# Two of four output-gate projection tiles moved from the matrix-LSTM stage into the attention stage of a hybrid decoder layer

## The chip, the core and the metric

The kernel runs on one core of one Trainium2 chip. The metric is the device time of one execution in microseconds; lower is better. The engines are TensorE (PE, its weight loads shown apart as PEld), VectorE (DVE), ScalarE (ACT), GpSimd (POOL) and SyncE (SP, which here only issues DMAs).

## The reference

One decoder layer over 1,024 positions of width 1,024, float32, batch 1. The attention has 8 heads of 64 (compressed, selected and window keys), the matrix-LSTM 4 heads of 128. The input is normalised and projected by one matrix of 3,360 columns; two groups of heads use parts of the result, are joined and projected back, and a memory attention and a gated MLP follow.

```python
h = rmsnorm(x, g_mix[l])
(nq, nkc, nvc, nks, nvs, nkw, nvw, ngt, mq, mk, mv, mo, mi, mf) = split_cols(h @ w_in[l], IN_SIZES)
o_nsa = nsa_batched(nq, ...)
qk = jax.nn.silu(causal_dwconv(jnp.concatenate([mq, mk], axis=-1), mlstm_conv_w[l]))
mq, mk = jnp.split(qk, 2, axis=-1)
h_m = mlstm_chunkwise(hd4(mq), hd4(mk), hd4(mv), mi + mlstm_b_i[l], mf + mlstm_b_f[l])
mixed = jnp.concatenate([head_rmsnorm(o_nsa, g_head_nsa[l]),
                         jax.nn.sigmoid(mo) * head_rmsnorm(h_m, g_head_mlstm[l])], axis=-1)
x = x + mixed @ w_out[l]
```

The part that matters here is `mo`: 512 columns, 128 for each of the four matrix-LSTM heads, whose sigmoid gates the normalised head. It depends on `h` alone, so it may be computed at any time after `h`.

## The kernel before

**Tiles.** Every projection is cut into tiles of 128 output columns. A tile of weights is loaded by SP (`load`, one of two slots in turn), split by POOL into a high and a low part (`split_tile`, L848 and L851) and multiplied on PE by the high and low parts of `h`, which stay in SBUF. One k-step of one half (512 positions) is three matmuls in `product` (L994, L997, L998); a tile is 2 halves x 8 k x 3 matmuls (`gemm_tile`). The order of the tiles is written by hand in `weight_tiles`, and all engines count along the same order with semaphores. POOL may overwrite a slot's split weights when PE has begun the tile after (`tile_started`); SP may load into a raw slot when its former tile is split.

**PSUM.** There are 8 banks of 512 columns. A ring hands them out: PE waits for `chunk_freed` before it opens a bank that is used again, DVE raises it when it has copied a bank out. During the attention the ring rests: scores use banks 0 to 3, transposes 4 and 5, sums 6 and 7.

**Attention (149 to 450 us of the span).** 128 head scores (4 heads x 2 branches x 16 blocks) and 164 steps (transposes of probabilities with the sums by values, and 16 turns of outputs) are interleaved in `NSA_ORDER`, an order made at build time from buffer space and a lag in columns; all engines walk it. For a score: PE `score_head` (L1144 to L1153) -> DVE maximum `shift_head` (L2196) -> ACT exponential `exp_head` (L1602) -> DVE reciprocal (L2208) -> POOL scaling (L876). PE may score head j when head j-2 has been exponentiated. For a step: PE four transposes `turn_block` (L1173, outputs L1164) -> ACT high part (L1622) -> DVE low part (L2004) -> PE two sums `sum_block` (L1192, L1193). The order begins with scores 0 to 9, one turn, score 10, two turns, scores 11 and 12. The last score (127) is followed by eleven steps, 153 to 163, of which 162 and 163 turn outputs and wait for a copy by ACT.

**Matrix-LSTM heads (450 to 700 us).** For each head PE runs the tiles of q, k, v and output gate in this order, then transposes `mv_feat` (L1035) as soon as DVE has copied the v tile, then the products of q and k in 12 pieces (L994 to L998 again, on `mq` and `mk`), then 72 matmuls of 129 columns with `tri` (L1250). DVE runs for q and for k: copy out (L2282), convolution over four taps (L2285, L2287), and after ACT's silu the low part (`mq_lo`, `mk_lo`, L2005); then `mv_feat` (L2301), the mask of the diagonal blocks (L2308), the copy of the output-gate tile into `o_gate` (L2311), the copy of the transposed v (L2314), and the pieces of `tri` (L2326, L2331) with decays that ACT makes (L1666, L1673). Then the head is normalised. ACT takes the sigmoid of `o_gate` behind the decays (L1676). `o_gate` lies over the keys of the attention, so nothing can be written there before the attention ends. Head 3 has 32 more transposes, of the attention's output, before its `tri` matmuls. The first 11 weight tiles are loaded before the attention begins; at its start the tile for head 0's q is split already, the one for k is loaded.

## Time and profile before

| | us |
|---|---|
| median of 3 runs | 1812.86 |
| lowest and highest run | 1810.57, 1812.99 |
| the profiled execution, its time | 1812.26 |
| its span (first to last instruction) | 1810.4 |

| engine | busy us | share of the span |
|---|---|---|
| PE | 1715.0 | 95% |
| PEld | 1417.8 | 78% |
| DVE | 1229.9 | 68% |
| ACT | 708.3 | 39% |
| POOL | 860.0 | 48% |

The profile is of one execution. Its page gives totals, the span in 40 slices and the costliest groups; the timeline gives each instruction with its start, its duration and, in brackets, how long its engine was idle before it and what released it. Starts are from the span's begin. Matmuls overlap: the duration of one is longer than the distance to the next, so distances between starts are used for sums. PEclk is the granted clock of PE as a share of 2.4 GHz.

### The profile page before, as it was taken

The page shows a single profiled execution, that of the slowest core. Times are in us where ns is not written, and L with a number is a line of the kernel's source. Part 1 is how long each engine was busy: PE and PEld are TensorE (multiplying, and loading weights), DVE is VectorE, ACT ScalarE, POOL GpSimd, SP SyncE. Part 2 cuts the span into 40 slices and gives each one's busy share as a digit, 9 for nine tenths or more (in the row PEclk, how much of TensorE's full clock was granted, in tenths as well). Part 3 has the DMA queues.
Part 4 walks back from the last instruction along what each step waited for, and adds up shares of the span by engine and source line. Part 5 has one row for each costly group of instructions (what it writes and reads, how often), then busy time and mean ns, then how long its engine had stood idle before and what let it go on. Part 6 is the DMA issues. An engine that isn't in the chain of part 4 may idle for free.

```text
span 1810.4 us, 23333 instructions
## 1 busy us (share of the span) xinstructions
PE 1715.0 (95%) x8416; PEld 1417.8 (78%) x8416; DVE 1229.9 (68%) x1641; ACT 708.3 (39%) x1326; POOL 860.0 (48%) x659
## 2 busy tenths in 40 slices
PE   7998899999999999989999898999999999999997
PEld 6886788877888887778777687777888888877886
DVE  6754677775887776446443532877888788789965
ACT  5114677776223324134111202433444443543444
POOL 3333344443433231410222243458988888679851
PEclk9998999998999999989999899999999999999999
DMA  5230011010111113114101022125533544695342
GB/s 189 82 117 13 24 36 36 28 44 1 58 47 36 36 59 128 47 38 151 57 23 35 24 82 93 35 82 199 191 125 120 175 144 144 207 330 181 118 133 93
DMA packets 78595, 170.07 MB, mean 94 GB/s; under 512 B 7644, under 2 KB 24220, under 8 KB 78368
## 3 DMA queue, kind: packets, MB, share of 16 engines
q1 hardware_dynamic: 67944, 135.71, 23.1%
q10 hardware_dynamic: 10552, 33.05, 4.8%
q8 instruction: 60, 0.98, 0.2%
q14 instruction: 39, 0.32, 0.1%
HBM read 133.06 MB, written 35.67 MB: 93 GB/s over the span
## 4 chain that ended last, share of the span: by engine, by line
PE 56%; DVE 17%; POOL 10%; ACT 7%; issue 7%; DMA 1%; ACTq 0%; SPq 0%; DVEq 0%; POOLq 0%
PE ps L994 13%; PE ps L998 13%; PE ps L997 13%; DVE x_t L2529 4%; PE ps L1173 3%; ACT x_t L1831 2%; POOL sum_s L905 2%; PE ps L1250 2%; POOL w_lo L899 2%; PE ps L1144 2%; PE ps L1334 2%; POOL w_lo L955 2%; DVE x_t L2558 2%; PE ps L1192 2%; DVE h_lo L2005 2%
## 5 line engine op out<-in xcount | busy, mean ns | idle before, releaser
L994 PE MATMUL ps<-h_hi,w_hi 128*128 128x512 f32 x1108 | 442.3, 399 | 17.2 <-DVE h_lo L2004 5.9
L997 PE MATMUL ps<-h_lo,w_hi 128*128 128x512 f32 x1108 | 436.8, 394 | 0.0
L998 PE MATMUL ps<-h_hi,w_lo 128*128 128x512 f32 x1108 | 436.8, 394 | 0.0
L848 POOL TENSOR_TENSOR w_hi<-w_raw,ones 128x1024 fp32r<-128x1024 f32 x55 | 113.9, 2070 | 619.2 <-PE ps L994 516.8
L994 PEld LDWEIGHTS ps<-h_hi,w_hi 128*128 128x128 f32 x1108 | 211.2, 191 | 71.1 <-ACT p_sum L1800 7.1
L998 PEld LDWEIGHTS ps<-h_hi,w_lo 128*128 128x128 f32 x1108 | 211.2, 191 | 44.8
L997 PEld LDWEIGHTS ps<-h_lo,w_hi 128*128 128x128 f32 x1108 | 211.7, 191 | 43.0 <-issue 0.7
L876 POOL TENSOR_SCALAR probs<-probs,nsa_inv,gate_sig 128x640 f32<-128x640 f32 (+7 forms) x128 | 100.2, 783 | 172.3 <-DVE nsa_inv L2208 172.3
L2529 DVE SCALAR_TENSOR_TENSOR x_t<-ps,par,x_t 128x1023 f32<-128x1023 f32 x84 | 107.7, 1282 | 80.2 <-ACT x_t L1831 78.7
L851 POOL TENSOR_TENSOR w_lo<-w_raw,w_hi 128x1024 fp32r<-128x1024 f32 x55 | 147.3, 2679 | 4.3
L2004 DVE TENSOR_TENSOR pt_lo<-ps,pt_hi 128x512 fp32r<-128x512 f32 (+1 forms) x148 | 101.8, 688 | 57.9 <-ACT pt_hi L1622 55.9
L1173 PE MATMUL ps<-ident,probs 128*128 128x128 f32 (+1 forms) x592 | 96.3, 288 | 12.1 <-POOL probs L876 6.6
L1622 ACT ACTIVATE pt_hi<-ps 128x512 fp32r<-128x512 f32 (+1 forms) x148 | 87.7, 596 | 45.8 <-PE ps L1173 45.1
L1602 ACT ACTIVATE probs<-ps,nsa_shift 128x640 f32<-128x640 f32 (+7 forms) x128 | 89.8, 702 | 38.6 <-DVE nsa_shift L2196 21.5
L2196 DVE TENSOR_REDUCE nsa_shift<-ps 128x1 f32<-128x640 f32 (+7 forms) x128 | 88.9, 698 | 16.2 <-PE ps L1153 11.2
L1173 PEld LDWEIGHTS ps<-ident,probs 128*128 128x128 f32 (+1 forms) x592 | 65.4, 141 | 25.2 <-DVE pt_lo L2004 11.1
L1144 PE MATMUL ps<-k_a,q_st 128*128 128x512 f32 (+3 forms) x192 | 71.2, 371 | 12.0 <-ACT probs L1602 7.5
L1710 ACT ACTIVATE sq<-x_t 128x1024 f32<-128x1024 f32 x16 | 17.0, 1061 | 147.0 <-DVE x_t L2373 80.5
L1760 ACT ACTIVATE xp<-ps,shift 128x256 f32<-128x256 f32 x32 | 15.0, 471 | 136.8 <-DVE shift L2473 136.8
L2004 DVE TENSOR_TENSOR z_lo<-h_part,z_hi 128x512 fp32r<-128x512 f32 x40 | 59.1, 1493 | 12.1 <-ACT z_hi L1878 12.1
L1145 PE MATMUL ps<-k_a,q_st 128*128 128x512 f32 (+3 forms) x192 | 65.7, 348 | 0.0
L899 POOL TENSOR_TENSOR w_lo<-w_raw,w_hi 128x512 fp32r<-128x512 f32 x38 | 51.4, 1352 | 29.3 <-ACT w_hi L1818 29.3
(360 smaller groups left out, 4079.2 us busy)
## 6 DMA issues: line engine op xcount, KB each, us to landing
w_raw<-in_w_tiles SPq DMA_DIRECT2D x109, 512.0 KB, 3.6
w_raw<-in_w_tiles SPq DMA_DIRECT2D x55, 256.0 KB, 3.0
s_new<-in_w_tiles SPq DMA_DIRECT2D x44, 256.0 KB, 4.0
z_dram<-x_t ACTq DMA_DIRECT2D x21, 512.0 KB, 2.9
b<-z_dram SPq DMA_DIRECT2D x33, 256.0 KB, 4.1
q_st<-q_dram SPq DMA_DIRECT2D x64, 128.0 KB, 2.9
t_dram<-t_new ACTq DMA_DIRECT2D x22, 256.0 KB, 5.2
s_dram<-s_new SPq DMA_DIRECT2D x22, 256.0 KB, 2.8
```

The costliest lines, as they stand in the source:

```text
L848: pool.tensor_tensor(w_hi[s][:, :], w_raw[s][:, :], ones[:, :].to_broadcast([P, KT * P]), ALU.mult).then_inc(w_hi_made.sem, w_hi_made.up())
L851: pool.tensor_tensor(w_lo[s][:, :], w_raw[s][:, :], w_hi[s][:, :].bitcast(FP32), ALU.subtract).then_inc(weights_split.sem, weights_split.up())
L876: ins = pool.tensor_scalar(row, row, nsa_inv[:, j % 8, br:br + 1], gate_sig[:, i, 3 * h + 1 + br:3 * h + 2 + br], ALU.mult, ALU.mult)
L994: ins = mm(out_ap, whi, x_hi, start=first, stop=False)
L997: mm(out_ap, whi, x_lo, start=False, stop=False)
L998: return mm(out_ap, wlo, x_hi, start=False, stop=last)
L1144: mm(o, qa, k_a[br][:, g, at_key:at_key + m], start=True, stop=False)
L1173: last = transpose(ps[0:width, 4 + k % 2, hd * P:hd * P + P], probs[:, at_p:at_p + width], ident[:, :])
L1602: ins = f(probs[:, P_AT[j]:P_AT[j] + n], flat[:, 0:n], ACT.Exp, bias=nsa_shift[:, j % 8, br:br + 1], accum_out=nsa_sums[:, j % 8, br:br + 1])
L2004: return tt(out_lo, src, hi.bitcast(FP32), ALU.subtract)
L2196: ins = dve.tensor_reduce(nsa_shift[:, j % 8, br:br + 1], flat[:, 0:n], AX.X, ALU.max, negate=True)
L2529: ins = stt(fc[p][i][:, k:SEQ], ps_flat[:, b:b + SEQ - k], conv_f[:, FTAPS - 1 - k, n:n + 1], fc[p][i][:, k:SEQ], ALU.mult, ALU.add)
```

## The change

The weight order becomes: output gates of heads 3 and 2 first, directly ahead of head 0's q; heads 0 and 1 keep four tiles, heads 2 and 3 have three.

The tile of head 3 is computed in eight portions (two k each, `fill_first`) in PSUM bank 7, behind scores 1, 2, 3, 4 (first half) and 6, 7, 8, 9 (second half). DVE copies each half, scaled, into `first_o`, behind its reductions of scores 6 and 11; PE starts the second half only after the first copy. `first_o` lies over a part of `o_nsa`, so ACT sends it by DMA to DRAM behind score 14, and from there into `o_gate` behind the attention.

The tile of head 2 is split by POOL in the middle of the attention (high part behind scaling 40, low part behind scaling 60), computed in eight portions (`fill_second`) in banks 0 and 1 behind steps 154 to 161, and copied by DVE into `o_gate` at the start of the matrix-LSTM stage.

```diff
+LAST_SCORE = max(n for n, (what, _) in enumerate(NSA_ORDER) if what == "s")
+FILL_AT = {1: (0, 0), 2: (0, 2), 3: (0, 4), 4: (0, 6), 6: (1, 0), 7: (1, 2), 8: (1, 4), 9: (1, 6)}
...
+    for h in (3, 2):
+        columns(win, C_MO + h * P)
     for h in range(MH):
-        for c in (C_MQ, C_MK, C_MV, C_MO):
+        for c in (C_MQ, C_MK, C_MV) + ((C_MO,) if h < 2 else ()):
...
+        first_o = at("first_o", FREE + 62 * KB, [P, SEQ])
+        o_dram = nc.dram_tensor("o_dram", (P, SEQ), FP32)
...
+                if j == 40:
+                    high_tile(0)
+                if j == 60:
+                    low_tile(0)
+
-            split_tile(0)
             split_pairs((FIRST_KV - 11) // 2)
...
+            def fill_second(c, k0, k1, slot):
+
+                for k in range(k0, k1):
+                    w = (w_hi[slot][:, k * P:k * P + P], w_lo[slot][:, k * P:k * P + P])
+                    ins = product(ps[:, c, :], w, h_hi[:, k, c * HALF:c * HALF + HALF], h_lo[:, k, c * HALF:c * HALF + HALF],
+                                  k == 0, k == KT - 1, tag=(c == 0 and k == 0))
+                if k1 == KT:
+                    ins.then_inc(chunk_done.sem, chunk_done.up())
+
+            fill_done = t("fill_done")
+            fill_slot = next_weights()
+
+            def fill_first(c, k0, k1):
+
+                if c and not k0:
+                    pe.wait_ge(t("fill_copied").sem, c)
...
+                    ins = product(ps[:, 7, :], w, h_hi[:, k, c * HALF:c * HALF + HALF], h_lo[:, k, c * HALF:c * HALF + HALF],
+                                  k == 0, k == KT - 1, tag=(c == 0 and k == 0))
...
+                if br == 0 and a == 0 and job == 1:
+                    pe.wait_ge(t("fill_copied").sem, 2)
...
                     score_head(z)
+                    if z in FILL_AT:
+                        c, k = FILL_AT[z]
+                        fill_first(c, k, k + 2)
...
+                    if at_order == LAST_SCORE + 2:
+                        fill_slot = next_weights()
+                        ring.resize(8)
+                        pe.wait_ge(head_exped.sem, HEADS)
+                    if LAST_SCORE + 2 <= at_order < LAST_SCORE + 10:
+                        n = at_order - LAST_SCORE - 2
+                        fill_second(n // 4, n % 4 * 2, n % 4 * 2 + 2, fill_slot)
...
-                gemm_tile(h_hi, h_lo)
-
-                pe.wait_ge(chunk_freed.sem, chunk_done.value(4))
+                if h < 2:
+                    gemm_tile(h_hi, h_lo)
+
+                pe.wait_ge(chunk_freed.sem, chunk_done.value(4 if h < 2 else 2))
...
+                    if z == 14:
+                        act.wait_ge(t("fill_copied").sem, 2)
+                        act.dma_start(o_dram[:, :], first_o[:, :]).then_inc(t("fill_moved", 16).sem, 16)
...
             act.wait_ge(ssq_ready.sem, ssq_ready.next())
+            act.wait_ge(t("fill_moved", 16).sem, 16)
+            act.dma_start(o_gate[:, 3, :], o_dram[:, :]).then_inc(t("fill_moved", 16).sem, 16)
...
+                if h == 3:
+                    act.wait_ge(t("fill_moved", 16).sem, 32)
...
+                    if g == 0 and i in (3, 4):
+                        dve.wait_ge(t("fill_moved", 16).sem, 16)
...
+            def copy_first(c):
+                dve.wait_ge(t("fill_done").sem, c + 1)
+                cs = slice(c * HALF, c * HALF + HALF)
+                tt(first_o[:, cs], ps[:, 7, :], r_in[:, cs], ALU.mult).then_inc(
+                    t("fill_copied").sem, t("fill_copied").up())
...
                     shift_head(n)
+                    if n in (6, 11):
+                        copy_first(n // 11)
...
+            b = chunk(2)
+            tt(o_gate[:, 2, :], both(b), r_in[:, :], ALU.mult).then_inc(chunk_freed.sem, chunk_freed.up(2))
             for h in range(MH):
...
-                b = chunk(2)
-                tt(o_gate[:, h, :], both(b), r_in[:, :], ALU.mult).then_inc(chunk_freed.sem, chunk_freed.up(2))
+                if h < 2:
+                    b = chunk(2)
+                    tt(o_gate[:, h, :], both(b), r_in[:, :], ALU.mult).then_inc(chunk_freed.sem, chunk_freed.up(2))
```

The eight semaphores `x_loaded0` to `x_loaded7` are given up, to make room for new ones; the loads of x use `block_loaded0` to `block_loaded7` instead, whose later values count one more.

## Rows read from the trace of the kernel before

**Rows 1.** The page, busy time of each engine and its share of the span
```profile
PE 1715.0 (95%) x8416; PEld 1417.8 (78%) x8416; DVE 1229.9 (68%) x1641; ACT 708.3 (39%) x1326; POOL 860.0 (48%) x659
```

**Rows 2.** Windows: length, busy PE, PEld, DVE, ACT, POOL, then PEclk, DMA share, GB/s
```profile
170.00:200.00 30.00, 22.79 (x138) 19.68 (x137) 17.34 (x44) 16.46 (x48) 10.53 (x16) 0.89 0.07 18
...
500.00:560.00 60.00, 60.00 (x318) 51.58 (x317) 45.84 (x70) 17.35 (x23) 19.09 (x8) 1.00 0.14 45
```

**Rows 3.** Timeline of PE, first scores: scores 2 and 10, and turn of step 3
```profile
153.87 0.33 PE L1144 MATMUL ps<-k_a,q_st 128*128 128x128 f32 x1 [2.68 <-ACT probs L1602]
...
165.85 0.50 PE L1144 MATMUL ps<-k_a,q_st 128*128 128x512 f32 x1 [0.54 <-ACT probs L1602]
...
174.87 1.09 PE L1173 MATMUL ps<-ident,probs 128*128 128x128 f32 x4 [3.77 <-POOL probs L876]
```

**Rows 4.** Windows; the last two of PE alone: length, busy PE, PEclk, DMA share, GB/s
```profile
154.00:158.00 4.00, 3.77 (x18) 3.58 (x18) 1.22 (x8) 1.63 (x9) 1.76 (x4) 0.51 0.01 2
...
444.00:448.00 4.00, 2.44 (x12) 0.95 0.00 0
...
450.00:454.00 4.00, 4.00 (x10) 0.50 0.00 0
```

**Rows 5.** Timeline of DVE, the reduction of a 128-column score
```profile
158.28 0.29 DVE L2196 TENSOR_REDUCE nsa_shift<-ps 128x1 f32<-128x128 f32 x1 [0.79 <-PE ps L1153]
```

**Rows 6.** Timeline of PE: step 154, step 162, head 0's first tile
```profile
435.81 0.60 PE L1173 MATMUL ps<-ident,probs 128*128 128x128 f32 x4
436.16 0.48 PE L1192 MATMUL ps<-pt_hi,v_hl 128*128 128x512 f32 x1
436.48 0.40 PE L1193 MATMUL ps<-pt_lo,v_hl 128*128 128x512 f32 x1
...
445.26 0.63 PE L1164 MATMUL ps<-ident,o_turn 128*128 128x128 f32 x4 [0.78 <-ACT o_turn L1630]
...
449.82 0.79 PE L994 MATMUL ps<-h_hi,w_hi 128*128 128x512 f32 x1 [0.93 <-DVE o_nsa L2218]
...
456.19 0.39 PE L994 MATMUL ps<-h_hi,w_hi 128*128 128x512 f32 x1
...
477.27 0.39 PE L994 MATMUL ps<-h_hi,w_hi 128*128 128x512 f32 x1
```

**Rows 7.** Timeline of DVE in head 1
```profile
534.08 1.23 DVE L2005 SCALAR_TENSOR_TENSOR mq_lo<-u_conv,mq_hi 128x1024 fp32r<-128x1024 f32 x1 [2.22 <-ACT mq_hi L1663]
...
546.26 1.95 DVE L2005 SCALAR_TENSOR_TENSOR mk_lo<-u_conv,mk_hi 128x1024 fp32r<-128x1024 f32 x1 [2.22 <-ACT mk_hi L1663]
548.14 1.21 DVE L2301 TENSOR_TENSOR mv_feat<-ps,r_in 128x1024 f32<-128x1024 f32 x1
549.28 3.19 DVE L2308 SCALAR_TENSOR_TENSOR u_conv<-m_bc,log_in,mmask 128x128 f32<-128x128 f32 x8
555.92 1.23 DVE L2311 TENSOR_TENSOR o_gate<-ps,r_in 128x1024 f32<-128x1024 f32 x1 [3.46 <-PE ps L998]
```

**Rows 8.** Timeline of PE in head 1: first product of q and k, then `tri`
```profile
556.45 0.47 PE L994 MATMUL ps<-mq_hi,mk_hi 128*128 128x512 f32 x1
...
563.10 8.26 PE L1250 MATMUL ps<-mv_tok,tri 128*128 128x129 f32 x72
```

**Rows 9.** Timeline of ACT and its DMA queue in heads 1 and 2
```profile
552.50 1.06 ACT L1666 ACTIVATE u_conv<-u_conv 128x1024 f32<-128x1024 f32 x1 [4.97 <-DVE u_conv L2308]
553.46 1.22 ACT L1673 ACTIVATE decay<-m_bc,log_in 128x384 f32<-128x384 f32 x2
...
579.75 0.33 ACTq L1657 DMA_DIRECT2D m_bc<-m_dram  x1
```

**Rows 10.** Timeline of POOL: scalings 41 and 61, first half of a split
```profile
247.43 0.98 POOL L876 TENSOR_SCALAR probs<-probs,nsa_inv,gate_sig 128x768 f32<-128x768 f32 x1 [1.41 <-DVE nsa_inv L2208]
...
291.44 0.88 POOL L876 TENSOR_SCALAR probs<-probs,nsa_inv,gate_sig 128x640 f32<-128x640 f32 x1 [2.24 <-DVE nsa_inv L2208]
...
545.24 1.89 POOL L848 TENSOR_TENSOR w_hi<-w_raw,ones 128x1024 fp32r<-128x1024 f32 x1 [5.72 <-PE ps L994]
```

More of the change, by code:

```diff
@@ L525, in build @@
             names[f"down_loaded{i}"] = ctx.enter_context(nc.semaphore(f"down_loaded{i}"))
-        for i in range(TT):
-            names[f"x_loaded{i}"] = ctx.enter_context(nc.semaphore(f"x_loaded{i}"))
         class View:
@@ L841, in _, with high_tile @@
             hi_made = w_hi_made
-            def split_tile(s):
+            def high_tile(s):
                 pool.wait_ge(loaded[s].sem, loaded[s].next())
@@ L849, in split_tile, with low_tile @@
                     w_hi_made.sem, w_hi_made.up())
+            def low_tile(s):
                 pool.wait_ge(w_hi_made.sem, w_hi_made.value())
@@ L853, in split_tile @@
                 tile_started.add(1)
+            def split_tile(s):
+                high_tile(s)
+                low_tile(s)
             def split_pairs(turns):
@@ L1115, in _ @@
             assert ring.bank() == FIRST_BANK
+            def fill_second(c, k0, k1, slot):
[10 more added lines that the diff above has]
+                    pe.wait_ge(t("fill_copied").sem, c)
+                for k in range(k0, k1):
+                    w = (w_hi[fill_slot][:, k * P:k * P + P], w_lo[fill_slot][:, k * P:k * P + P])
+                    ins = product(ps[:, 7, :], w, h_hi[:, k, c * HALF:c * HALF + HALF], h_lo[:, k, c * HALF:c * HALF + HALF],
+                                  k == 0, k == KT - 1, tag=(c == 0 and k == 0))
+                if k1 == KT:
+                    ins.then_inc(fill_done.sem, fill_done.up())
             def score_head(j):
@@ L1196, in _ @@
             summed = 0
-            for what, z in NSA_ORDER:
+            for at_order, (what, z) in enumerate(NSA_ORDER):
                 if what == "s":
                     score_head(z)
+                    if z in FILL_AT:
+                        c, k = FILL_AT[z]
+                        fill_first(c, k, k + 2)
                 else:
@@ L1511, in x_high @@
             def x_high(k):
-                act.wait_ge(t(f"x_loaded{k}", 16).sem, t(f"x_loaded{k}", 16).next())
+                act.wait_ge(t(f"block_loaded{k}", 16).sem, t(f"block_loaded{k}", 16).next())
                 f(h_hi[:, k, :], x_f[:, k, :], ACT.Copy, scale=gains[:, G_MIX, k:k + 1]).then_inc(
@@ L1655, in _ @@
             ring.resize(8)
+            chunk_done.add(2)
             for h in range(MH):
@@ L1663, in _ @@
                     f(hi[:, :], u_conv[:, :], ACT.Copy, scale=scale).then_inc(hi_ready.sem, hi_ready.up())
-                chunk_done.add(8 + 2 + 2 + (2 if h else 0))
+                chunk_done.add((8 if h < 2 else 6) + 2 + 2 + (2 if h else 0))
                 act.wait_ge(diag_ready.sem, diag_ready.next())
@@ L1868, in down_highs @@
                     block_loaded = t(f"block_loaded{k}", 16)
-                    block_loaded.n = {0: 1, 1: 2, 3: 3, 5: 5, 6: 4}[n]
+                    block_loaded.n = {0: 1, 1: 2, 3: 3, 5: 5, 6: 4}[n] + (k < KT)
                     act.wait_ge(block_loaded.sem, block_loaded.value())
@@ L2602, in z_sum @@
                 block_loaded = t(f"block_loaded{k}", 16)
-                block_loaded.n = 3 if n == 2 else 4
+                block_loaded.n = (3 if n == 2 else 4) + (k < KT)
                 dve.wait_ge(block_loaded.sem, block_loaded.value())
```

5 lines of the change are left out of this document (2 added, 3 removed).

## The prediction

> **What bounds the kernel now.** I read the page's totals first: TensorE (PE) is busy 95% of the span, VectorE (DVE) 68% [rows 1]. A change that moves PE work pays only if it moves it from where PE is the limit to where PE waits. So next comes the table by stretches [rows 2]: at the start of the attention PE is busy 22.8 of 30 us; in the matrix-LSTM heads 60.0 of 60, and DVE 45.8.
>
> The change takes one of the four projection tiles out of heads 2 and 3, where PE never rests, and lays both tiles into the attention. Two questions decide: how much of each tile falls into gaps there, and whether a head without it is shorter by the whole tile or meets another wait first. They need PE's timeline at both places of the attention [rows 3, 6] and DVE's, PE's and ACT's in a head [rows 7 to 9].
>
> **Price of a tile.** 93 matmuls of 512 columns, 31 groups of three, start between 456.19 and 477.27 [rows 6]: 0.227 us each. A tile is 2 halves x 8 x 3 = 48 of them, 10.9 us; a portion of two k is 6, 1.36 us, and twice that where the granted clock is 0.5.
>
> **First tile, eight portions behind scores 1 to 4 and 6 to 9.** Score 2 starts at 153.87 after 2.68 us of waiting for ACT [rows 3]; the portion behind score 1 fits into that wait and is free. From 154 to 158 PE is busy 3.77 us of 4, at a granted clock of 0.51, that is 1.2 GHz [rows 4]: hardly a gap is left, only slow matmuls. Score 10 starts at 165.85, 12.0 us behind score 2; less 0.54 of waiting [rows 3], 0.5 for the turn before it and some 0.3 of smaller gaps that is 10.7 of slow scores, 5.3 at full clock.
> The new length: scores 5.3, seven portions 9.5, the turn 0.5. PE is idle most of the time until 153.87 still, so I let the clock fall at 154 and come back after one dense portion: 1.6. The portion behind score 6 needs the bank that DVE empties only after it has reduced score 6: 0.29 and a little more for the reduction [rows 5], 0.6 to 0.7 for a 128x512 copy (half of the 1.21 of a 128x1024 one, [rows 7]), with the hand-overs 1.4 in which PE waits; score 7 and all behind it stand in its queue. Sum 18.3 against 12.0: +6.3. The second copy stands on DVE between the reductions of scores 11 and 12, ahead of the reciprocal that POOL, and then the turn at 174.87 with its idle time of 3.77, wait for [rows 3]: +0.5. For a further short fall of the clock in the copy wait, +0.7. First tile **+7.5**. Ends: +3.3 (no fall of the clock, copy wait hidden) and +10.9 (nothing hidden). I see nothing later that absorbs it: in the attention PE, ACT, DVE and POOL wait for one another, and so shift together.
>
> **Second tile, eight portions behind the last turns.** A turn is four transposes (0.35), then two sums (0.32, and some 0.24) [rows 6]: 0.91. From 435.81 to 445.26, less the 0.78 of waiting before it, there are eight steps, 1.08 each, so only 0.17 a step and those 0.78 are open. From 436.9 there remain 7 x 0.91 = 6.4 plus 10.9: the turn of 445.26 moves to 454.2, **+8.9**. The tail, 445.26 to 449.82 [rows 6], stays. In it PE was busy 2.44 of 4 us, and from 450 to 454 head 0's first tile ran at a granted clock of 0.50 [rows 4], a loss of 2. Behind denser work it may fall later: I take off 0.9. Second tile **+8.0**; ends +6.7 and +10.9. It also puts one DVE copy of 1.2 ahead of head 0, where its banks are emptied. That costs nothing, since DVE waits 3.46 us for the output-gate tile in head 0 as in head 1 [rows 7]; without that cover it would cost 1.2.
>
> **POOL and DMAs.** The second tile's split goes behind POOL's scalings 40 and 60. POOL idles 1.41 us ahead of scaling 41 and 2.24 ahead of 61; the first half of a split takes 1.89 (545.24), the second I bound by twice that [rows 10]. So a scaling starts up to 1.5 us late and the next, with idle times of their own, are on time: 0, at most 2. The split for head 0's first tile may start once the second tile has started, 17 us ahead of need. The two DMA issues on ACT cost about 0.33 of its queue each (a like issue, [rows 9]), the second ahead of the root that DVE waits for, but under the cover of head 0. The data are back long before head 3. Together **+0.3**. SP loads one tile per split as before, in another order of columns.
>
> **Heads 2 and 3 without their tile.** In head 1 DVE reads the fourth tile at 555.92 [rows 7], so the third ends at about 545.0. DVE ends mv_feat, which frees the third tile's bank for PE's transposes, at 549.35, works to 552.5 on the mask, idles 3.46 for the fourth tile, copies it (1.15) and goes on [rows 7]. Without the tile PE waits for mv_feat. POOL's split from 545.24 [rows 10], beside which mk_lo takes 1.95 where mq_lo takes 1.23 [rows 7], moves up to the third tile's start: 0.7 gained. DVE gains 3.46 + 1.15 + 0.7 = 5.3, less 0.45, as ACT's first decay is ready only 1.6 us behind the mask (552.50 to some 554.1, [rows 9]): the products that fill tri start 4.85 earlier. PE's 72 small matmuls behind them [rows 8], held by DVE first and dense after, end some 5.1 earlier, not 10.9. In head 3 the part before them hangs on DVE wholly: 4.8. Together **-9.9**; ends -7 and -21.8. Half of each removed tile turns into PE waiting for DVE.
>
> **Sum.** 7.5 + 8.0 + 0.3 - 9.9 = +5.9. The profiled execution took 1812.26 us, 1.9 more than its span of 1810.4; the median of three runs is 1812.86, 0.6 above it. 1812.3 + 5.9 = **1818.2**.
>
> **A rule weighed.** The rows say: 2.68 us idle, then a granted clock of 0.51; 2.44 busy of 4 until 448, then 0.50 [rows 3, 4]. The Trainium skill, "TensorE: Matmul & The Clock Gate", Part 1, says that the throttled state is the default and activity releases it. For the first tile this speaks for the change: the portions would hold the clock up, and the sum would be the second rival's. For heads 2 and 3, with a new idle time of about 4 us, it speaks against it: the third rival's.
>
> **Rivals.**
> 1. *Heads bound by PE.* PE shows 60.0 of 60 busy [rows 2]. If DVE's chain closes up once the tiles come sooner, both tiles vanish whole: 7.5 + 8.0 + 0.3 - 21.8 = -6.0, 1806.3. It decides where mv_feat ends less than 1 us behind the third tile; against it, it ends 4.4 behind. Chance 0.13.
> 2. *The clock stays up.* The first portion fills the wait before 153.87, the scores run at 2.4 GHz and the copy wait is half hidden: first tile +4.0, second +6.9, sum +1.3, 1813.6. For it: the half-rate stretch is there to be won. Against: 2.44 busy of 4 did not hold the clock at 448 [rows 4]. Chance 0.24.
> 3. *New falls of the clock.* After the idle time in heads 2 and 3 the products ahead of tri (6.65 us from 556.45 to 563.10, [rows 8]) run at half rate and DVE waits for them; the copy wait lowers the clock in the scores again: savings -7, first tile +10, sum +11.3, 1823.6. For it: shorter waits than those 4 us lowered the clock at 154 and 450 [rows 4]. Against: DVE and ACT take the products at a slower pace than PE makes them, so they have a lead to lose. Chance 0.18.
> 4. The forecast, 0.45.
>
> **How the numbers follow.** About 0.2% (3.6 us) is what a measurement can tell from no change. Rival 1 and a sliver of 2 are faster: 0.15. Most of rival 2 and a sixth of the forecast, whose open terms spread it by some 3 us each way, are within: 0.29. The rest is slower: 0.56. The range goes from the forecast to rival 2's better side and rival 3's centre, leaving out rival 1 and the top of rival 3: 1810 to 1824.5.
>
> **What would show it.** Right: score 10 starts 5 to 8 us later; head 0's first tile starts at about 465; the output-gate copies of heads 0 and 1 stay 60 apart, the heads 2 and 3 take about 55; PE idles 4 us before the transposes of mv_feat there, released by DVE. Wrong: granted clock 1.0 from 154 to 162 (rival 2); a head of about 49 us (rival 1); clock 0.5 under the products of heads 2 and 3 and DVE waiting for PE (rival 3).

## The result and the profile after

The changed kernel took 1822.43 us (median) beside 1812.72 for the kernel before: a ratio of 1.0056, 95% interval 1.0031 to 1.0080. Five of its six executions lie at 1821.91 to 1823.82; the sixth took 2155 us at a mean granted clock of 0.747 and is left out of the ratio. In a later session it was 1821.05 beside 1811.54, ratio 1.0053 (1.0041 to 1.0066). So it is some 10 us slower, where the forecast said +5.9 and 1818.2, with a range to 1824.5. It moved the way that was forecast and ended inside the range. The size was 4 us short, and the runs below show which terms made that up.

The page's busy times, to be laid beside [rows 1]. The work is the same; DVE has one operation more, as the first tile is copied in two halves.

```profile
PE 1715.6 (94%) x8416; PEld 1417.5 (78%) x8416; DVE 1229.8 (68%) x1642; ACT 708.3 (39%) x1326; POOL 859.8 (47%) x659
```

The span is 1820.5 against 1810.4. I followed the offset between the two traces at matching operations, that is, how much later the same operation starts in the changed kernel:

| place (time before) | after less before | step |
|---|---|---|
| score 1 (150.64) | +1.2 | ahead of any portion |
| score 10 (165.85) | +6.1 | first tile, its portions: +4.9 |
| turn of step 3 (174.87) | +6.5 | |
| DVE's low part 24 (224.25) to 437 | +11.4 to +11.8 | what came behind it: +5.2 |
| head 0's first tile (449.82) | +20.8 | second tile: +9.1 |
| o_gate tile of head 1 (555.92) | +23.8 | head 0: +3.0, head 1: 0 |
| end of head 2 | +18.4 | -5.4 |
| end of head 3 | +12.3 | -6.1 |
| end | +10.1 | -2.2 |

Below, an offset "at step 8, 12 or 24" is that of DVE's low part of this number (at 185, 196 and 224 us in before); a "turn" is PE's.

Timeline of PE in the changed kernel, for [rows 3]: score 2, the first matmul of the tile's second half, score 10, the turn of step 3.

```profile
155.12 0.33 PE L1180 MATMUL ps<-k_a,q_st 128*128 128x128 f32 x1 [1.26 <-ACT probs L1650]
...
163.24 0.49 PE L1007 MATMUL ps<-h_hi,w_hi 128*128 128x512 f32 x1 [1.11 <-DVE first_o L2286]
...
172.00 0.48 PE L1180 MATMUL ps<-k_a,q_st 128*128 128x512 f32 x1
...
181.34 1.09 PE L1209 MATMUL ps<-ident,probs 128*128 128x128 f32 x4 [3.87 <-POOL probs L886]
```

The first portion lay in the wait (1.26 left of 2.68), the second half waited 1.11 us for the copy, and PE's wait for POOL before step 3 is as long as ever. Windows of PE alone, for [rows 4] (length, busy PE, granted clock, DMA share, GB/s):

```profile
154.00:158.00 4.00, 2.88 (x16) 1.00 0.01 2
158.00:162.00 4.00, 4.00 (x28) 1.00 0.02 4
182.00:186.00 4.00, 4.00 (x15) 0.50 0.00 0
186.00:190.00 4.00, 4.00 (x18) 0.56 0.00 0
```

The clock stays at 2.4 GHz where it was 0.51 before, but behind the wait for POOL it is at or near 1.2 GHz for some eight us, where the profile of before shows one window of four at 0.57 (below, with experiment 6). At the end of the attention, where [rows 4] have 2.44 busy of 4 us and then 0.50, it does not fall: PE is busy 2.29 of 4 us from 467 to 471, and the clock reads 1.00 there and in the four behind. The end of the attention, for [rows 6]: step 162 and head 0's first tile.

```profile
466.57 0.60 PE L1200 MATMUL ps<-ident,o_turn 128*128 128x128 f32 x4
...
470.64 0.50 PE L1007 MATMUL ps<-h_hi,w_hi 128*128 128x512 f32 x1 [0.93 <-DVE o_nsa L2276]
```

Head 0, on ACT's queue, on DVE and on PE, with a window of PE behind its wait. This is the stretch that the prediction had down as covered.

```profile
479.53 0.33 ACTq L1705 DMA_DIRECT2D o_gate<-o_dram  x1
479.89 1.28 ACT L1706 ACT_TABLE_LOAD   x1 [9.77 <-DVE ssq L2311]
```
```profile
481.48 0.55 DVE L2315 RECIPROCAL rstd<-rstd 128x64 f32<-128x64 f32 x1 [1.98 <-ACT rstd L1706]
482.06 8.81 DVE L2318 TENSOR_TENSOR o_nsa<-o_nsa,rstd 128x512 f32<-128x512 f32 x8
...
516.56 1.22 DVE L2369 TENSOR_TENSOR mv_feat<-ps,r_in 128x1024 f32<-128x1024 f32 x1
...
519.79 1.22 DVE L2380 TENSOR_TENSOR o_gate<-ps,r_in 128x1024 f32<-128x1024 f32 x1
```
```profile
517.84 1.97 PE L1048 MATMUL ps<-ident,mv_feat 128*128 128x128 f32 x8 [3.38 <-DVE mv_feat L2369]
```
```profile
517.00:521.00 4.00, 3.17 (x12) 0.57 0.00 0
```

For head 0 of the kernel before, the line that answers to the o_gate copy:

```profile
495.90 1.22 DVE L2311 TENSOR_TENSOR o_gate<-ps,r_in 128x1024 f32<-128x1024 f32 x1 [3.47 <-PE ps L998]
```

DVE now reaches the o_gate tile with no wait at all, where it waited 3.47 us before, as in head 1 [rows 7]. PE waits 3.38 us for mv_feat in a head that still has all four tiles, and the clock falls to 1.2 GHz behind that wait. The cover, the waiting of DVE in which the prediction hid the copy and the issues, was used up.

Head 2, the DVE operations that answer to [rows 7], and PE's wait:

```profile
630.09 1.23 DVE L2061 SCALAR_TENSOR_TENSOR mk_lo<-u_conv,mk_hi 128x1024 fp32r<-128x1024 f32 x1 [2.21 <-ACT mk_hi L1717]
...
632.37 2.18 DVE L2376 SCALAR_TENSOR_TENSOR u_conv<-m_bc,log_in,mmask 128x128 f32<-128x128 f32 x8
...
636.25 0.29 DVE L2395 TENSOR_TENSOR tri<-ps,u_conv 128x128 f32<-128x128 f32 x1 [0.50 <-ACT decay L1727]
```
```profile
632.51 1.30 PE L1048 MATMUL ps<-ident,mv_feat 128*128 128x128 f32 x8 [3.77 <-DVE mv_feat L2369]
```

Here the forecast's picture stands: mk_lo takes 1.23 where it took 1.95, the wait of 3.46 and the copy are gone, ACT's first decay costs 0.50, and PE idles 3.77 us for DVE. The mask too lost the split on POOL that ran beside it (2.18 for 3.19), which the forecast had left out.

### The profile page after: what moved, and what is told of

The parts are those of the page before. It is cut to its first block, busy times and chain, and to the rows that moved or that the text cites. A ratio compares the mean times of both kernels' runs of the same rounds, so it can differ in the third digit from the quotient of the medians.

```text
span 1820.5 us, 23339 instructions
## 1 busy us (share of the span) xinstructions
PE 1715.6 (94%) x8416; PEld 1417.5 (78%) x8416; DVE 1229.8 (68%) x1642; ACT 708.3 (39%) x1326; POOL 859.8 (47%) x659
## 4 chain that ended last, share of the span: by engine, by line
PE 50%; DVE 21%; POOL 10%; ACT 8%; issue 8%; DMA 1%; ACTq 0%; SPq 0%; DVEq 0%; POOLq 0%
PE ps L1007 11%; PE ps L1010 11%; PE ps L1011 11%; DVE x_t L2598 4%; PE ps L1209 3%; ACT x_t L1887 2%; POOL sum_s L918 2%; DVE u_conv L2355 2%; POOL w_lo L912 2%; PE ps L1382 2%; DVE x_t L2627 2%; DVE h_lo L2061 2%; PE ps L1180 2%; PE ps L1230 2%; POOL w_lo L968 1%
## 5 line engine op out<-in xcount | busy, mean ns | idle before, releaser
L1209 PE MATMUL ps<-ident,probs 128*128 128x128 f32 (+1 forms) x592 | 97.3, 289 | 12.3 <-POOL probs L886 6.9
L1209 PEld LDWEIGHTS ps<-ident,probs 128*128 128x128 f32 (+1 forms) x592 | 66.8, 143 | 24.7 <-issue 11.4
L1180 PE MATMUL ps<-k_a,q_st 128*128 128x512 f32 (+3 forms) x192 | 70.1, 365 | 9.6 <-ACT probs L1650 5.4
L1230 PE MATMUL ps<-pt_hi,v_hl 128*128 128x512 f32 x132 | 65.0, 493 | 0.0
```

The source lines that it names most:

```text
L1180: mm(o, qa, k_a[br][:, g, at_key:at_key + m], start=True, stop=False)
L1209: last = transpose(ps[0:width, 4 + k % 2, hd * P:hd * P + P], probs[:, at_p:at_p + width], ident[:, :])
L1230: mm(o, v, pt_hi[k % 3][0:e, :], start=br == 0 and a == 0, stop=False)
```

## The experiments

Theory at the start: the parts of the table above add up, each with its price. Rivals: that what came behind score 10 is not the tile's but the clock's, drawn anew in each execution; that head 0's loss is the order on ACT's queue. Ratios are against the kernel before on the same chip, with 95% intervals.

**1. The first tile alone** (head 3's tile; head 2 computes its own again; no copy of a gate ahead of head 0, head 0's split back behind the scalings).

```
-    for h in (3, 2):
+    for h in (3,):
...
-                if h < 2:
+                if h not in (3,):
                     gemm_tile(h_hi, h_lo)
```

> The changed kernel with head 3's output-gate tile alone moved (between the first scores, copied to DRAM and back); head 2 computes its own as before, nothing is laid between the last turns, POOL splits head 0's first tile after its last scaling as before. Theory (the parts add up as the trace of after reads): +10.5 in the attention, of which 6 stand at score 10 and the rest comes from longer falls of the clock by step 40, head 3 -6, head 0 at nothing because its wait for the o_gate tile is back: +4.5 against before, between +3 and +6. Rival (the rest beyond score 10 is how the falls of the clock happen to lie in one execution, not the price of the tile): offset at score 10 of 5 to 6 and no more behind, total -1 to +1.

Measured: 1815.98, ratio 1.0030 (1.0017 to 1.0043), +5.4 us or so. Attention +11.1, head 0 to 1 +1.8, head 3 -5.6, all against the first profile of before. The total lies in the theory's range, but head 0 was not at nothing: PE waits there without a second tile in the kernel. The rival is out by its total; by experiment 6 it was right about 4 of the 11.1.

```profile
506.80 1.97 PE L1045 MATMUL ps<-ident,mv_feat 128*128 128x128 f32 x8 [2.54 <-DVE mv_feat L2357]
```

**2. The second tile alone** (the same edits for head 2, without the first tile and its two DMAs).

```
-                    if z in FILL_AT:
-                        c, k = FILL_AT[z]
-                        fill_first(c, k, k + 2)
...
-            act.dma_start(o_gate[:, 3, :], o_dram[:, :]).then_inc(t("fill_moved", 16).sem, 16)
```

> Head 2's output-gate tile alone moved, between the last turns; the first scores are those of before, and no DMA of a gate. Theory: +9.0 in the last turns, head 0 at 0 to +1.3 (the copy of the gate ahead of it, mostly under its 3.46 us of waiting, which the second tile's place leaves there), head 2 -5.4: +4.3, between +3.5 and +5.5; the attention's steps up to 435 us as before within 1. Rival A (the tile's price is the clock: head 0's first tile ran at half rate before and does not now): +7 in the turns, total +2. Rival B (head 0 is the place where it is lost, whatever was moved first): head 0 +3 again, total +7.

Measured: 1818.78, ratio 1.0053 (1.0036 to 1.0069), +9.6 by the ratio, more than any theory said. The profiled execution was the quickest of the six, 1816.06; in it the turns cost +9.6 and head 2 gave 4.3 back. Its surprise is at the start: with nothing of the change in the first scores, it stands -0.4 at score 10, +2.9 at step 8, +4.8 at step 24 and +5.0 by 250 us against the first profile of before. That is the growth of the changed kernel, +5.2 from score 10 to step 24. So it is not the tile's.

**3. The load behind the root.**

```
-            act.wait_ge(t("fill_moved", 16).sem, 16)
-            act.dma_start(o_gate[:, 3, :], o_dram[:, :]).then_inc(t("fill_moved", 16).sem, 16)
             f(rstd[:, :, 0:NH], ssq[:, :, 0:NH], ACT.Sqrt, scale=1.0 / DH, bias=EPS).then_inc(
                 std_ready.sem, std_ready.up())
+            act.wait_ge(t("fill_moved", 16).sem, 16)
+            act.dma_start(o_gate[:, 3, :], o_dram[:, :]).then_inc(t("fill_moved", 16).sem, 16)
```

> The changed kernel with one edit: ACT issues the load of o_gate from DRAM behind the root of the NSA norms, not ahead of it. Theory: the root comes 1.3 to 1.65 us earlier, and as head 0 now has no wait left on DVE, all behind it comes as much earlier; the scaling of o_nsa also no longer lies beside the load: 1.5 to 3 us faster than the changed kernel, so +7 to +8.5 against before. Rival A (the root hides under another wait, POOL's split or PE): no difference to the changed kernel, +9 to +10. Rival B (the slow scaling of o_nsa is POOL's split beside it, so it stays 8.8 us): only the 1.65 are gained.

Measured: 1819.99, ratio 1.0051 (1.0029 to 1.0073): no gain by the median. The profile (an execution of 1812.53) shows what the order does, on ACT and on DVE:

```profile
476.18 0.26 ACT L1704 ACTIVATE rstd<-ssq 128x64 f32<-128x64 f32 x1 [8.10 <-DVE ssq L2311]
476.19 0.33 ACTq L1707 DMA_DIRECT2D o_gate<-o_dram  x1
```
```profile
476.47 0.56 DVE L2315 RECIPROCAL rstd<-rstd 128x64 f32<-128x64 f32 x1 [0.32 <-ACT rstd L1704]
477.06 8.80 DVE L2318 TENSOR_TENSOR o_nsa<-o_nsa,rstd 128x512 f32<-128x512 f32 x8
```

The root's table load is no longer in the chain and the wait is 0.32 as it was before, 1.66 less. The scaling still takes 8.80 (rival B), and it does in experiment 2 too, where no gate is loaded. Its eight operations, read one at a time, show why: six take 0.68 or 0.69 each, and two take this:

```profile
480.69 2.38 DVE L2318 TENSOR_TENSOR o_nsa<-o_nsa,rstd 128x512 f32<-128x512 f32 x1
...
482.99 2.88 DVE L2318 TENSOR_TENSOR o_nsa<-o_nsa,rstd 128x512 f32<-128x512 f32 x1
```

They are the two beside the halves of POOL's split, which lie at 480.39 (2.13 us) and 482.60 (2.72). Every profile with a scaling of 8.80 has exactly one such pair, and it moves with the split. In before (4.91) the split starts at 463.46, when six of the eight are done; the last two take 0.69, and here the split's first half is the long one, 2.79. No PE wait for mv_feat is left in head 0 here.

This profile's span is 10.3 us below the changed kernel's, but that is not all the order's: 3.6 lie in head 0, 2.3 near 435 us, where the clock did not fall in this execution, and 4.2 behind head 3.

**4. Six spare matmuls in the first wait**, into a bank that nobody reads.

```
                     score_head(z)
+                    if z == 1:
+                        pe.wait_ge(weights_split.sem, weights_split.n + 1)
+                        for k in range(2):
+                            w = (w_hi[1][:, k * P:k * P + P], w_lo[1][:, k * P:k * P + P])
+                            product(ps[:, 7, :], w, h_hi[:, k, 0:HALF], h_lo[:, k, 0:HALF], k == 0, k == 1)
```

> The kernel before with six matmuls more behind score 1, into a bank that nobody reads there: they take 1.4 us of a wait of 2.7 us. They move nothing. Theory (the wait lets the clock fall to half, and work in it holds the clock up): granted clock 1.0 from 154 to 162, score 10 some 4 to 5 us earlier; of this 0 to 4 us arrive at the end, as later falls of the clock take some of it back. Rival A (the clock falls for what PE did before 138, not for this wait): no difference. Rival B (the cost of first falls is given back wholly by ACT's and DVE's own pace behind score 10): score 10 earlier, the end the same within 1.

Measured: 1811.74, ratio 1.0010 (0.9998 to 1.0021): nothing. The granted clock read 0.91 from 154 to 158 and 0.50 from 158 to 162: the fall came 3 us later, not never. Score 10 stood 0.9 earlier, and later falls took that back (+2.3 by 250 us). One portion in the wait does not hold the clock; in the changed kernel each following score had its portion, and there it held. A finding by the way: this kernel has nothing of the change in head 0, but its first tile runs there at full clock, and of DVE's wait for the o_gate tile 0.43 is left.

```profile
495.87 1.23 DVE L2316 TENSOR_TENSOR o_gate<-ps,r_in 128x1024 f32<-128x1024 f32 x1 [0.43 <-PE ps L998]
```

**5 and 6. Both kernels a second time, unedited.**

> The changed kernel once more, unedited, on the chip of the runs below, for a second profile of the same program. Theory (when the clock falls is drawn anew in each execution, and the offset of +11.7 in the attention held some of it): against the profile of before the score 10 stands +4 to +6 again, but the steps behind it and the tail differ from the first profile by up to 3 us where a fall lies elsewhere; PE's wait for mv_feat in head 0 is there again. Rival (the falls belong to the program): each offset the same within 0.5.

> The kernel before once more, unedited, for a second profile. Theory: head 1 to the end of head 3 the same within 0.5; between 154 and 240 us the steps later than in the first profile by 2 to 5 us, as they are in the kernels that share this code (the one with the second tile alone, +5.1; the one with six spare matmuls, +2.3), or the first dense head at full clock where the first profile showed it at half. Rival (those offsets came from the edits): each step the same within 0.5.

Measured: the changed kernel 1821.05, the one before 1811.67 (ratio to itself 0.9999, 0.9989 to 1.0009). Windows of PE alone in the second profile of **before**:

```profile
154.00:158.00 4.00, 3.04 (x16) 0.67 0.01 2
178.00:182.00 4.00, 4.00 (x15) 0.50 0.00 0
194.00:198.00 4.00, 3.94 (x17) 0.50 0.02 4
222.00:226.00 4.00, 4.00 (x15) 0.50 0.02 4
```

The same stretches in the first profile of before, the one with the forecast's rows:

```profile
174.00:178.00 4.00, 3.13 (x11) 0.57 0.00 0
190.00:194.00 4.00, 2.00 (x8) 0.70 0.20 59
214.00:218.00 4.00, 1.86 (x7) 0.69 0.00 0
```

One program has a window wholly at 1.2 GHz after each of three waits in one execution, and a shorter fall each time in the other. It stands +4.2 by step 24 and keeps that to the end of the heads, though its total is 0.8 less than the first's (it lost less elsewhere). The second profile of the changed kernel stands +11.0, so the second pair differs by 6.8 where the first pair differs by 11.7. What follows is the same in both pairs up to head 3: second tile +9.6 at the output turn of step 162, head 2 -5.4, head 3 -6.1 and -6.2. Behind head 3, in code that no edit touches, the second profile of before is 5.2 quicker than the first. The theory of falls drawn anew is confirmed for before; for after, the two profiles lie 0.7 apart in the attention.

**7. Experiment 1 with the load behind the root.**

> The kernel with head 3's tile alone moved, and the load of o_gate from DRAM behind the root. Theory (the issue ahead of the root and its table load delays DVE's chain in head 0 past the cover): PE's wait of 2.54 us for mv_feat in head 0 and the short fall of the clock behind it go, -3 against the kernel with head 3's tile alone, so +2 to +3 against before. Rival (it needs the second tile too): the wait stays and the time is +5.4.

Measured: 1812.66, ratio 1.0007 (0.9996 to 1.0018). Against the 1.0030 of experiment 1 that is 4.2 us for two lines in another order. Each of the two ratios is known to some 2 us each way; the profiles put 4.4 of it into head 0. DVE in head 0:

```profile
499.89 1.22 DVE L2357 TENSOR_TENSOR mv_feat<-ps,r_in 128x1024 f32<-128x1024 f32 x1
...
503.62 1.23 DVE L2368 TENSOR_TENSOR o_gate<-ps,r_in 128x1024 f32<-128x1024 f32 x1 [0.41 <-PE ps L1008]
```

From the squaring of o_nsa to mv_feat DVE takes 38.3 us in before, 45.1 in experiment 1, 40.2 here, 45.9 in the changed kernel and 41.4 in experiment 3. The order of the issue is worth 4.9 or 4.6 of that, though only 1.66 is the root's wait. The rest lies in the two convolutions of q and k, which meet POOL's splits in another way in the slow cases; experiment 11 comes back to it. The gate's copy ahead of head 0 is the 1.15 between 40.2 and 41.4. Of the 3.46 of cover, 0.41 is left here; PE's first tile, at full clock now and not at half as in [rows 4], took some 2 of it from the other side.

**8. The first tile in finer places**, with experiment 7 (head 3's tile alone, the load behind the root) as its base: a portion where PE waits, in the size of the wait, one k behind each score between, and two banks, so that no copy is waited for. DVE makes the copies behind the reciprocals of the scores and not ahead of them.

```
-FILL_AT = {1: (0, 0), 2: (0, 2), 3: (0, 4), 4: (0, 6), 6: (1, 0), 7: (1, 2), 8: (1, 4), 9: (1, 6)}
+FILL_AT = {1: (0, 0, 4), 2: (0, 4, 5), 3: (0, 5, 6), 4: (0, 6, 7), 5: (0, 7, 8), 6: (1, 0, 1), 7: (1, 1, 2), 8: (1, 2, 3), 9: (1, 3, 4), 12: (1, 4, 8)}
...
-                if c and not k0:
-                    pe.wait_ge(t("fill_copied").sem, c)
...
-                    ins = product(ps[:, 7, :], w, h_hi[:, k, c * HALF:c * HALF + HALF], h_lo[:, k, c * HALF:c * HALF + HALF],
+                    ins = product(ps[:, 6 + c, :], w, h_hi[:, k, c * HALF:c * HALF + HALF], h_lo[:, k, c * HALF:c * HALF + HALF],
...
-                    if n in (6, 11):
-                        copy_first(n // 11)
                     if inverted < begun:
                         invert_sums(inverted)
                         inverted += 1
+                    if n in (6, 12):
+                        copy_first(n // 12)
```

> As the one above, but the tile lies in other places: four k behind score 1 (2.7 us, the length of the wait there), one k (0.68 us) behind each of scores 2 to 9, four k behind score 12, where PE waited 3.77 us for POOL; the halves in banks 6 and 7, so that nothing waits for a copy. Theory (the price of the first tile is set by its places: two portions in waits, the rest against the half-rate stretch): score 10 at 0 to +2, the turn of step 3 at 0 to +2, head 3 -6: -4 against before, between -6 and -1. Rival A (scores, exponentials and reductions are in step, so that any matmul between them costs its time): +5 at score 10, total 0 to +1. Rival B (the clock falls all the same and the portions run at half rate): +5 and more at the turn, total +2 or more.

Measured: 1803.44, ratio **0.9960** (0.9947 to 0.9972), 8 us faster than before, 9 faster than experiment 7, and better than its range. PE in this kernel: the turn of step 3, and the windows around it.

```profile
175.01 0.63 PE L1204 MATMUL ps<-ident,probs 128*128 128x128 f32 x4 [0.97 <-POOL probs L886]
```
```profile
174.00:178.00 4.00, 3.02 (x19) 1.00 0.00 0
178.00:182.00 4.00, 4.00 (x30) 1.00 0.00 0
182.00:186.00 4.00, 4.00 (x31) 1.00 0.03 6
```

The turn is 0.1 later than in before, with all 48 matmuls (10.9 us) ahead of it, and the wait before it is 0.97. No fall follows this wait; the next comes behind 190 us. By 196 us the kernel is 1.5 ahead of the first profile of before, by 250 us 0.8 behind; from the last turns to the end of head 0 it gains 2.6, in head 3 5.3.

**9. Experiment 3 once more, for its profile.**

> The changed kernel with the load behind the root, unedited a second time: its first seven runs lay at 1812.5 to 1813.4 (three) and 1820.0 to 1824.3 (four), and its profile was one of the low ones. Theory (a high one differs by falls of the clock in and behind head 0, which a low one doesn't have): a profile near 1820 shows one or two stretches more at a granted clock near 0.5 between 450 and 720 us, each worth 2 to 3 us, with the attention's offsets the same within 2. Rival (the attention itself has two courses): the offset at the last turns differs by 5 or more. If the profile is a low one again, this stays open.

Measured: 1821.83, ratio 1.0054 (1.0039 to 1.0068), and the profile was again one of the low ones (1813.1). With those of experiment 3, 5 of 17 times lie at 1812.5 to 1813.4 and 12 at 1818.7 to 1824.3. None of the 12 was profiled, but the mean granted clock of every execution is on record: 0.978 in each of the five, 0.973 to 0.976 in the 12. So the 12 spent more time at 1.2 GHz. As an estimate from these figures, 0.003 less over 1812 us is 11 us more at half rate, which can cost up to 5.4 of the 8 us. Where it lay is open. In the low profiles head 0 takes 3.6 less than in the changed kernel, close to the 4.4 of experiment 7.

**10. Both tiles, the first in finer places, the load behind the root** (experiments 3 and 8 in one).

> The first tile in its finer places, the load behind the root, and head 2's tile between the last turns as in the changed kernel. Theory (the second tile's places hide nothing): against the kernel with the first tile alone in these places, +9.0 in the turns, +1 in head 0, -5.5 in head 2, so +4 to +5: -4 against before, between -6 and 0. Rival A (it costs all of its 10.9 and head 2 gives nothing in a typical run, as the +9.6 of the kernel with the second tile alone would have it): +9 to +10 on the one with the first tile alone, so +1 to +2 against before. Rival B (with the head's DVE chain no longer behind, it pays): 0 or less on it.

Measured: 1805.28, ratio 0.9975 (0.9961 to 0.9990). Nine of twelve times lie at 1803.1 to 1808.4, three at 1812.4 to 1813.1. So it beats before by 4.5, but not experiment 8: the second tile takes away 3 us. In the profile it costs 7.3 in the turns and 1.6 in head 0 against experiment 8, and head 2 gives 5.7: +3.2, near the 2.7 by the ratios. The 7.3 is the +9.6 of the other profiles less 2.3, as the clock did not fall near 430 us in this one.

**11. The second tile two steps later.**

```
-                    if LAST_SCORE + 2 <= at_order < LAST_SCORE + 10:
-                        n = at_order - LAST_SCORE - 2
+                    if LAST_SCORE + 4 <= at_order < LAST_SCORE + 12:
+                        n = at_order - LAST_SCORE - 4
```

> As the one above, with the eight portions of head 2's tile two steps later, behind the turns of steps 156 to 163, so that the last two lie in PE's waits of 0.78 and 0.93 us at the end of the attention. Theory (two waits more are filled): 1.7 less than the one above, up to 4 less where the fall of the clock in those waits goes too. Rival (head 0's first tile then waits for DVE or for its split weights instead): no difference.

Measured: 1808.41, ratio 0.9985 (0.9974 to 0.9996), 3 us more than number 10, not less. The second tile costs 6.1 up to the last output turn for the 7.3 of number 10, so part of the waits was filled. But head 0 then takes 2.9 more. DVE (q's convolution: its last three operations, then the slow ones of them alone) and POOL (the split beside it), in number 10 and then here:

```profile
479.05 5.44 DVE L2352 SCALAR_TENSOR_TENSOR u_conv<-u_raw,par,u_conv 128x1024 f32<-128x1024 f32 x3
...
481.69 2.80 DVE L2352 SCALAR_TENSOR_TENSOR u_conv<-u_raw,par,u_conv 128x1024 f32<-128x1024 f32 x1
```
```profile
481.39 2.02 POOL L852 TENSOR_TENSOR w_hi<-w_raw,ones 128x1024 fp32r<-128x1024 f32 x1 [6.00 <-PE ps L1007]
483.49 3.28 POOL L857 TENSOR_TENSOR w_lo<-w_raw,w_hi 128x1024 fp32r<-128x1024 f32 x1
```
```profile
479.36 7.45 DVE L2352 SCALAR_TENSOR_TENSOR u_conv<-u_raw,par,u_conv 128x1024 f32<-128x1024 f32 x3
...
480.68 2.80 DVE L2352 SCALAR_TENSOR_TENSOR u_conv<-u_raw,par,u_conv 128x1024 f32<-128x1024 f32 x1
...
483.51 3.30 DVE L2352 SCALAR_TENSOR_TENSOR u_conv<-u_raw,par,u_conv 128x1024 f32<-128x1024 f32 x1
```
```profile
480.27 2.13 POOL L852 TENSOR_TENSOR w_hi<-w_raw,ones 128x1024 fp32r<-128x1024 f32 x1 [5.77 <-PE ps L1007]
482.47 3.26 POOL L857 TENSOR_TENSOR w_lo<-w_raw,w_hi 128x1024 fp32r<-128x1024 f32 x1
```
```profile
504.14 1.97 PE L1048 MATMUL ps<-ident,mv_feat 128*128 128x128 f32 x8 [2.49 <-DVE mv_feat L2366]
```

POOL's splits follow PE's tiles, so they came earlier against DVE: 0.9 us behind the start of the three operations instead of 2.3. An operation of the convolution takes 1.29 alone. In number 10 one is slowed, to 2.80, beside the split's first half; the second half lies under the 2.22 us in which DVE waits for ACT anyway. Here both halves meet an operation, 2.80 and 3.30. q's convolution takes 2.0 us more, k's behind it 1.8 more, and PE's wait for mv_feat is back. Experiments 1 (the split 0.2 us behind, 7.45) and 7 (1.8 behind, 5.44) fall on the same two sides. In the changed kernel the split comes still earlier: from the copy of q to that of k it takes 12.9 us, for 10.8 in experiment 3. So a shift of a microsecond or two between POOL and DVE tips head 0 by up to 4 us, and that is what the order of the issue did. The profiles agree on it operation by operation; no run moved POOL alone. Neither expectation was right: the rival named the right engine, but for a wait, not for slower operations.

**12. The wait for POOL opened again** in the kernel of experiment 8.

```
-FILL_AT = {1: (0, 0, 4), 2: (0, 4, 5), 3: (0, 5, 6), 4: (0, 6, 7), 5: (0, 7, 8), 6: (1, 0, 1), 7: (1, 1, 2), 8: (1, 2, 3), 9: (1, 3, 4), 12: (1, 4, 8)}
+FILL_AT = {1: (0, 0, 4), 2: (0, 4, 5), 3: (0, 5, 6), 4: (0, 6, 7), 5: (0, 7, 8), 6: (1, 0, 1), 7: (1, 1, 2), 8: (1, 2, 3), 9: (1, 3, 8)}
```

> The kernel with the first tile in its finer places, with one edit: the four k behind score 12 are laid behind score 9 instead, so that PE's wait for POOL before the turn of step 3 stands open again. Theory (of the 9 us between coarse and finer places some 4 are falls of the clock that this open wait brings): the turn of step 3 at +2.5 to +3, and a granted clock near 0.5 for some 8 us behind it, so +3.5 to +4 more by 196 us: +6 to +7 on the finer one, -2 to -1 against before. Rival (the wait is filled for nothing but its own length): the turn +2.7, no longer fall behind it, +2.7 in all, -5.5 against before.

Measured: 1809.38, ratio 1.0003 (0.9988 to 1.0017): against the 0.9960 of experiment 8 that is 7.8 us lost for the place of twelve matmuls, 2.7 us long (each ratio to some 2 us each way, on two chips). PE's turn of step 3 and the windows, to be laid beside those of experiment 8:

```profile
178.34 1.08 PE L1204 MATMUL ps<-ident,probs 128*128 128x128 f32 x4 [3.78 <-POOL probs L886]
```
```profile
174.00:178.00 4.00, 0.56 (x6) 0.77 0.00 0
178.00:182.00 4.00, 3.66 (x12) 0.50 0.00 0
182.00:186.00 4.00, 4.00 (x16) 0.50 0.00 0
```

The turn is 3.3 later, and by step 12 (196 us) the kernel is 7.6 behind experiment 8. So the length of the wait is 3.3 and the half rate that follows it some 4. The theory stands and was a little too mild; the rival's 2.7 falls.

## Why the prediction was right or wrong

**First tile, +7.5.** Score 10 stood at +6.1 for the +6.3 forecast, and PE's wait for the copy was 1.1 for 1.4. The near hit of the 6.3 is luck. It held 1.6 for a fall of the clock at 154 that did not come (rival 2's mark, a granted clock of 1.0 from 154 to 162, was there), and score 1 already stood 1.2 late, ahead of any portion. From score 2 to score 10 all profiles with these portions take 16.9 us, for 12.0 and 11.8 in before: +4.9 or +5.1. How late score 1 stood varied from -0.65 to +1.25 between the profiles of kernels with the same code up to there.

The step that failed in this term is "I see nothing later that absorbs it", in its unsaid other half: that nothing later adds. The offset grew to 11.4 in the first pair of profiles. In the second pair it ends at 6.8, because the kernel before itself varies by 4.2 in this stretch with how long its clock stays down after the waits from about 171, 190 and 214 on. What is left of the growth in the second pair is 1.5: behind the wait for POOL the changed kernel's clock is low for longer (0.50 from 182 to 186 and 0.64 to 190 in its second profile) than that of before. The first profile of before, on which all sums stood, was a good draw there. 7.5 lies between the two pairs, and the total of 4 us too little can't be laid on this term alone.

**The clock in the first scores.** The forecast gave 0.24 to "the clock stays up" and bet on a fall at 154. The Trainium skill, "TensorE: Matmul & The Clock Gate", Part 1, has the throttled state as the default, from which activity releases; by that rule the stretch would be won, and the trace agrees, with 1.00 from 154 to 162. It was worth little, since the next open wait, 3.87 us for POOL, was followed by a fall anyway. Experiment 4 filled half of the first wait alone and gained nothing; experiment 12 shows that the wait for POOL was one to fill.

**Second tile, +8.0.** The turns cost +9.6 at step 162 for the 8.9 forecast, and the tail gave back about 0.5 where I took off 0.9: +9.1. The mechanism was right, the size off by 1. The clock near 430 us is apart from this: where it did not fall, the kernel gained 2.3 there.

**POOL and DMAs, +0.3, and head 0.** This is the step that failed plainly. The two issues were priced at 0.33 each, "under the cover of head 0", and the same cover of 3.46 was given to the gate's copy. Head 0 took +3.0. From the squaring of o_nsa to mv_feat DVE's chain grew by 7.6 us:

- 3.9: the scaling of o_nsa, 8.81 for 4.91, two of its operations beside POOL's split. The prediction had nothing for it.
- 1.7: the issue ahead of the root kept ACT's table load in the chain (1.98 of waiting for 0.32).
- 1.15: the gate's copy.
- 0.9: k's convolution. q's takes 12.9 us up to the next copy both before and after.

Reading the cover in head 1 was no fault: before has 3.47 in head 0. But that wait hung on PE's first tile at half rate [rows 4], and the same prediction took 0.9 off because this fall might go. In experiment 4 it goes, with no gate moved: PE is 2.1 us quicker through the tiles, the scaling is long, and 0.43 of the cover is left. So the cover was spent twice, and most of it goes when that tile runs at full clock, as it did in the changed kernel. Experiments 1 and 7 show that the order of the issue alone is worth 4.2, most of it by the convolutions (experiment 11). I had priced a queue entry by its length and not by what stands behind it. With both tiles in the kernel the same edit saves 3.6 in head 0 of the profiles, but nothing by the median (experiments 3 and 9), so there its net worth is not shown.

**Heads 2 and 3, -9.9.** Measured -5.4 and -6.1. The mechanism is the one forecast: PE idles 3.8 us for mv_feat, half of a tile turns into waiting. The mask's 3.19 shrank by 1.0 with POOL's split gone from beside it; that was not in the sum. Rival 1 (-21.8) is out in every run. Rival 3's fall shows weakly (0.57 from 633 to 637 in head 2) and cost no saving there. In experiment 2 it was longer (0.50 from 621 to 625, 0.66 to 629), and head 2 gave 4.3.

**The sum.** In the first pair of profiles +11.7, +9.1, +3.0 and -11.5 make 12.3, and -2.2 follows behind head 3, which no part of the change explains; unedited code varies there by 5.2. In the second pair +6.8, +9.3, +2.8 and -11.6 make 7.3, and the end stands at +7.9, where the medians say +9.7 and +9.5. There the terms set beside the forecast's 7.5, 8.0, 0.3 and -9.9 are off by -0.7, +1.3, +2.5 and -1.7: the largest is head 0. The time was nearest to rival 3's 1823.6, for reasons that were mostly not its own.

What stays open: where the kernels with the second tile and the load behind the root lose 8 us in some executions. These have the lower granted clock (experiment 9), but none was caught in a profile; that head 0 is tipped to its slower side in them, which would be 4 of the 8, is a guess. Open with it is the net price of the second tile, +9.6 alone, some +4 in the changed kernel (1.0053 less the 1.0030 of the first tile alone), +3 in experiment 10.

## What to carry to other kernels

Put filler in the size of a wait and into the waits, not evenly: with the same 48 matmuls experiments 7 and 8 lie 9 us apart by their places and those of the two copies, and twelve of them in one wait of 3.8 us were worth 7.8. Before an instruction is put ahead of another on a queue, ask what the second one has to do first (a table load). Charge each use against a cover once, in the stretch where it lies, and ask what makes the cover: here it hung on a slow tile. When a group of operations is slow, read them one at a time: here only the two beside POOL's split were slow. Take a second profile of the same kernel before reading offsets of a few us: unedited code differed by 4.2 us within 80 us of trace.

## What was unexpected of the hardware

- A granted clock once at 1.2 GHz cost more than the wait before it: 3.3 us of wait and some 4 of half rate (experiment 12). How long it stayed low after like waits varied between executions of one program: 0.57 for one window, or a whole window at 0.50 with parts of its neighbours (experiment 6).
- One dense portion in an open stretch delayed a fall by 3 us and did not prevent it (experiment 4).
- DVE's scaling of o_nsa took 8.80 instead of 4.91 us for the same eight operations. Six took 0.68 each as ever; the two that met the halves of POOL's split took 2.38 and 2.88 (experiment 3). In before, PE's first tile at half rate had kept the split away until 463.46. In experiment 4, which has none of the change's work in head 0, that tile ran at full clock, and the scaling took 8.80 too: a faster PE moved POOL's work beside DVE's.
- The convolution of q took 5.44 or 7.45 us for three operations. A half of a split made one operation of 1.29 into 2.80 or 3.30, and the shorter case is the one in which the second half fell into DVE's own wait for ACT (experiments 10 and 11).
